# Second mixer: mLSTM output with tokens on partitions, and the large products of a beat in one run

## What is computed

```python
Dm = jnp.where(causal, b[..., :, None] - b[..., None, :] + ig[..., None, :], -jnp.inf)
m = jnp.maximum(bq, jnp.max(Dm, axis=-1))
Wt = jnp.exp(Dm - m[..., None]) * jnp.einsum('bhcld,bhcsd->bhcls', qc, kc)
num = inter[..., None] * jnp.einsum('bhcld,bhcdv->bhclv', qc, Cs) + jnp.einsum('bhcls,bhcsv->bhclv', Wt, vc)
den = inter * jnp.einsum('bhcld,bhcd->bhcl', qc, ns) + jnp.sum(Wt, axis=-1)
h = num / jnp.maximum(jnp.abs(den), jnp.exp(-m))[..., None]
```

## Time and profile before

| | us |
|---|---|
| median of 3 runs | 1571.99 (1571.65 to 1573.32) |
| profiled execution | 1571.24 |
| its span | 1569.5 |
| TensorE busy | 1549.0, 99% |
| VectorE busy | 1001.8, 64% |
| ScalarE busy | 705.1, 45% |
| GpSimd busy | 180.9, 12% |

### The profile page before, as it was taken

One profiled execution on the slowest core, in us unless ns is written; L12 is line 12 of the kernel. 1 busy time (PEld: TensorE's weight loads), 2 busy tenths in 40 slices (PEclk: granted clock), 3 DMA queues, 4 the chain that ended last, 5 costly groups with the idle time before them and its releaser, 6 DMA issues.

```text
span 1569.5 us, 20966 instructions
## 1 busy us (share of the span) xinstructions
PE 1549.0 (99%) x7858; PEld 1266.9 (81%) x7858; DVE 1001.8 (64%) x1861; ACT 705.1 (45%) x1386; POOL 180.9 (12%) x167
## 2 busy tenths in 40 slices
PE   8999999999999999999999999999999999999998
PEld 8888888888876888888888888767667888888887
DVE  7876667544778577767653377676776655554356
ACT  7544444423556555444442343344444443433254
POOL 0221122100004202221120000000011011110000
PEclk9999999999999999999999999999999999999999
DMA  5333333334151313333333424221101333333332
GB/s 212 94 104 93 100 101 95 107 95 141 56 151 25 98 38 108 94 100 90 98 101 94 143 95 137 68 48 48 48 28 61 95 93 100 95 98 98 95 113 68
DMA packets 91973, 146.21 MB, mean 93 GB/s; under 512 B 9056, under 2 KB 30944, under 8 KB 91744
## 3 DMA queue, kind: packets, MB, share of 16 engines
q1 hardware_dynamic: 89392, 139.07, 29.8%
q10 hardware_dynamic: 2480, 5.80, 1.2%
HBM read 140.12 MB, written 2.10 MB: 91 GB/s over the span
## 4 chain that ended last, share of the span: by engine, by line
PE 91%; DVE 5%; issue 1%; ACT 1%; DMA 1%; SPq 0%; POOL 0%; DVEq 0%; POOLq 0%
PE ps L452 24%; PE ps L454 24%; PE ps L453 24%; PE ps L2039 2%; PE ps L2041 1%; PE ps L2040 1%; PE ps L491 1%; PE ps L492 1%; PE ps L493 1%; PE ps L1763 1%; PE ps L1743 1%; PE ps L1722 1%; PE ps L1378 1%; PE ps L1409 1%; PE ps L473 1%
## 5 line engine op out<-in xcount | busy, mean ns | idle before, releaser
L437 DVE TENSOR_TENSOR wl<-raw,wh 128x512 fp32r<-128x512 f32 (+2 forms) x419 | 303.7, 729 | 391.5 <-ACT wh L428 390.7
L428 ACT ACTIVATE wh<-raw 128x512 fp32r<-128x512 f32 (+2 forms) x419 | 260.8, 627 | 539.3 <-PE ps L454 534.5
L452 PE MATMUL ps<-Hh,wh 128*128 128x512 f32 x1088 | 426.1, 392 | 2.2 <-DVE st L1830 1.9
L454 PE MATMUL ps<-Hh,wl 128*128 128x512 f32 x1088 | 423.5, 389 | 0.0
L453 PE MATMUL ps<-Hl,wh 128*128 128x512 f32 x1088 | 423.4, 389 | 0.0
L452 PEld LDWEIGHTS ps<-Hh,wh 128*128 128x128 f32 x1088 | 204.1, 188 | 46.0 <-DVE Hl L2328 2.1
L454 PEld LDWEIGHTS ps<-Hh,wl 128*128 128x128 f32 x1088 | 204.1, 188 | 42.8
L453 PEld LDWEIGHTS ps<-Hl,wh 128*128 128x128 f32 x1088 | 204.2, 188 | 42.0
L452 PE MATMUL ps<-AH,wh 128*128 128x512 f32 x416 | 161.8, 389 | 0.0
L453 PE MATMUL ps<-AL,wh 128*128 128x512 f32 x416 | 161.8, 389 | 0.0
L454 PE MATMUL ps<-AH,wl 128*128 128x512 f32 x416 | 161.8, 389 | 0.0
(11 more groups left out here) (352 smaller groups left out, 2236.3 us busy)
## 6 DMA issues: line engine op xcount, KB each, us to landing
raw<-in_w_in SPq DMA_DIRECT2D x216, 256.0 KB, 2.7
raw<-in_w_out SPq DMA_DIRECT2D x104, 256.0 KB, 2.6
raw<-in_w_up SPq DMA_DIRECT2D x64, 256.0 KB, 2.7
raw<-in_w_down SPq DMA_DIRECT2D x32, 256.0 KB, 2.7
raw<-in_w_q SPq DMA_DIRECT2D x16, 256.0 KB, 2.8
raw<-in_w_o SPq DMA_DIRECT2D x16, 256.0 KB, 3.2
raw<-in_w_pg SPq DMA_DIRECT2D x16, 256.0 KB, 2.6
X<-in_xT SPq DMA_DIRECT2D x8, 256.0 KB, 4.6
```

Of the source, the lines that this page charges most:

```text
L428: e.activation(split_in[n][0][:, 0:width], raws[n % NRAW][:, 0:width], ACT.Copy, scale=1.0 if gain is None else gain).then_inc(s_hi, 1)
L437: e.tensor_tensor(wl[:, 0:width], raw, wh[:, 0:width].bitcast(F32), ALU.subtract).then_inc(s_lo, 1)
L452: e.matmul(b, wh[:, o:o + w], xh, start=k == 0, stop=False, skip_group_check=joined)
L454: m = e.matmul(b, wl[:, o:o + w], xh, start=False, stop=k == (nk - 4 if closing else nk - 1), skip_group_check=joined)
```

## The change

The output of an mLSTM head is now made with tokens on partitions: the decayed scores are the weights and the values are streamed, with a column of ones beside them (`mvt` is 129 of 132 wide), so that the sum of the weights comes out as column 128. Blocks 0 to 2 of tokens go to bank 3, block 3 (step 5) to bank 2. The squares are summed by ScalarE with `accum_out`; the two Abs follow. `dve_lstm_diag` scales the rows on VectorE (384 and 128 columns of PSUM), and step 7 transposes the four blocks back, after which VectorE multiplies with the gate out of PSUM. The additions on GpSimd and VectorE, the products with ones and the copy of the output go away.

TensorE's order in a beat is `unit`, `sums`, both groups of transposes, the `lstm` step, and then all large products of the beat. Thirty beats hold two halves, four hold one, beats 34 and 35 none; the `lstm` steps begin in beat 6. VectorE takes a tile at the start of the next beat. All tiles of the inputs go to bank 0. Bank 1 is for the transposes of group 1; units with one or two blocks put both groups into bank 6, and ScalarE copies both at once. Head 3's output moves ahead of the attention's last two in the order of `w_out`.

```diff
+        mvt = sub("b_mvt", [P, 2, 4, 132], o_)
...
-        W_ORDERS = ((0, 1, 4, 5, 6, 2, 3, 7), (0, 1, 2, 4, 5, 6, 3, 7))
+        W_ORDERS = ((0, 1, 4, 5, 6, 7, 2, 3), (0, 1, 2, 4, 5, 6, 3, 7))
...
-        M_FIRST = {b: ("m", b, 0) for b in range(29)}
-        M_SECOND = {b: ("m", b, 1) for b in range(29)}
-        M_SECOND.update({29 + i: ("m", 29 + i // 2, i % 2) for i in range(6)})
...
-            MIX += second_half + [("turn", b)] + [("mtake", t // 2)] * (t % 2 and half) + step
-            if b >= 8 and (b % 8 < 2 and b < 32 or b in (34, 35)):
-                MIX += [("mo", b // 8 - 1, b % 8 % 2)]
+            at_ = sum(RUN[:b])
+            run = halves[at_:at_ + RUN[b]] if b < NU else [("w0", b - NU)]
+            lane = b - LSTM_AT
+            step = [("lstm", *LSTM[lane])] if 0 <= lane < 32 else []
+
+            MIX += made + [("unit", b)]
+            MIX += [("lstm_diag", lane // 8)] * (0 <= lane < 32 and lane % 8 == 7)
+            MIX += [("lstm_exp", *LSTM[lane - 1])] * (1 <= lane <= 32 and (lane - 1) % 8 < 4)
+            MIX += run + [("turn", b)] + step
+            if lane >= 3 and (lane % 8 in (3, 4) and b < 30 or b in (35, 36)):
+                MIX += [("mo", 3 if b > 30 else lane // 8, (lane + 1) % 2 if b < 30 else b - 35)]
             if b > 32:
                 MIX += [("fill", b - 33)]
-
-            if b < 5:
-                PE_MIX += (first_half if b == 0 else []) + [("unit", b)] + (first_half if b else [])
-                PE_MIX += [("turn0", b)] + second_half + [("turn", b)]
-            elif b < 29:
-                PE_MIX += [("unit", b), ("sums", b), ("turn0", b)] + first_half + den + [("turn", b)] + second_half + step
+            made = [("mtake", t // 2) for what, t, half in run if t % 2 and half] if b < NU else []
+
+            if b == 0:
+                PE_MIX += run[:1] + [("unit", b)] + run[1:]
+            elif b < 5:
+                PE_MIX += [("unit", b)] + run + [("turn", b)]
             elif b < NU:
-                PE_MIX += [("unit", b), ("sums", b), ("turn0", b)] + den + second_half + [("turn", b)] + step
+                PE_MIX += [("unit", b), ("sums", b), ("turn", b)] + step + run
             else:
-                PE_MIX += [("w0", b - 35)] * (b == NU + 2) + [("turn0", b), ("sums", b)] + den
-                PE_MIX += second_half + [("turn", b)] + step
-        MIX += [("lstm_diag", 3), ("fill", 6), ("w0", 4), ("w0", 5), ("lstm", *LSTM[31]), ("w0", 6), ("fill", 7), ("w0", 7)]
-        PE_MIX += [("w0", 4), ("w0", 5), ("lstm", *LSTM[31]), ("w0", 6), ("w0", 7)]
+                PE_MIX += [("sums", b), ("turn", b)] + step + run
+        MIX += [("w0", 3), ("fill", 6), ("w0", 4), ("fill", 7), ("w0", 5), ("w0", 6), ("w0", 7)]
+        PE_MIX += [("w0", c) for c in range(3, 8)]
...
+        def short(u):
+
+            return u >= 4 and UNITS[u][1] < 2
...
+        def turn_bank(u, g):
+
+            return turned[6][:, 256 * g:] if short(u) else turned[(6, 1)[g]]
...
                 tb = UNITS[u][1]
+                bank = turn_bank(u, g)
                 if g == 0:
                     e.wait_ge(s_nm, u + 1)
                     if u > 0:
-                        e.wait_ge(s_cp1, u)
-                else:
-                    e.wait_ge(s_cp0, u + 1)
+                        e.wait_ge(s_cp0, u)
+                elif not short(u) and second_copies(u) > 1:
+                    e.wait_ge(s_cp1, second_copies(u) - 1)
...
-                    e.activation(unit_t(u, 0)[:, 0:L], turned[6][:, 0:L], ACT.Copy).then_inc(s_cp0, 1)
+                    if short(u):
+                        i = (0, 4)[u % 2]
+                        e.activation(tall[:, i:i + 2, 2:2 + L], turned[6].rearrange("p (g c) -> p g c", g=2)[:, :, 0:L],
+                                     ACT.Copy).then_inc(s_cp0, 1)
+                    else:
+                        e.activation(unit_t(u, 0)[:, 0:L], turned[6][:, 0:L], ACT.Copy).then_inc(s_cp0, 1)
...
+            if 0 <= u < NU and not short(u):
                 tb = UNITS[u][1]
...
         LT, LB, LN = [T[2], T[3], T[6], T[7]], turned[2], turned[3]
-        DECAY = (LT[1], LT[2], LT[3], LT[2])
...
                 e.wait_ge(s_mm, 4 * h + i + 1)
                 if i == 0:
                     e.wait_ge(s_mtc, h + 1)
-                e.matmul(LN[:, n0:S], mvt[:, h, i, :], DECAY[i][:, n0:S], start=i == 0, stop=i == 3,
-                         skip_group_check=True).then_inc(s_ma, 1)
-            if s == 6:
-                e.wait_ge(s_msq, h + 1)
+                for tb in range(i, 3):
+                    m = e.matmul(LN[:, LD * tb:LD * tb + LD], DECAY[i][:, (tb - i) * P:(tb - i + 1) * P],
+                                 mvt[:, h % 2, i, 0:LD], start=i == 0 and tb == 0, stop=i == tb, skip_group_check=True)
+                if i == 2:
...
+            if s == 5:
+                e.wait_ge(s_mm, 4 * h + 4)
+                for i in range(4):
+                    m = e.matmul(LB[:, 0:LD], DECAY[i][:, (3 - i) * P:(4 - i) * P], mvt[:, h % 2, i, 0:LD], start=i == 0,
+                                 stop=i == 3)
+                m.then_inc(s_ma, 1)
+            elif s == 7:
+                e.wait_ge(s_mrow, h + 1)
                 for tb in range(4):
-                    m = e.matmul(LB[:, 8 + tb:9 + tb], LT[2][:, tb * P:(tb + 1) * P], ones[:, 0:1], start=False,
-                                 stop=True, skip_group_check=True)
-                m.then_inc(s_mden, 1)
-            elif s == 7:
-                e.wait_ge(s_mdx, h + 1)
-                for tb in range(4):
...
-                e.activation(mvt[:, h, :, :], LN[:, :].rearrange("p (n c) -> p n c", n=4), ACT.Copy).then_inc(s_mtc, 1)
...
-                e.wait_ge(s_mres, h + 1)
-                e.activation(LT[2], big[:, MQ + h, :], ACT.Square).then_inc(s_msq, 1)
-            elif s == 6:
-                e.wait_ge(s_mden, h + 1)
                 if h > 1:
-                    e.wait_ge(s_mdx, h - 1)
-                e.activation(lane_col(h, 0), LB[:, 0:4], ACT.Abs).then_inc(s_mabs, 1)
+                    e.wait_ge(s_mrow, h - 1)
+                for tb in range(4):
+                    if tb % 3 == 0:
+                        e.wait_ge(s_ma, 2 * h + 1 + tb // 3)
+                    e.activation(LT[(3, 1)[tb // 2]][:, tb % 2 * P:(tb % 2 + 1) * P], l_rows(tb), ACT.Square, accum_out=lane_col(h, 2)[:, tb:tb + 1])
+                e.activation(lane_col(h, 0)[:, 0:3], LN[:, 0:3 * LD].rearrange("p (b c) -> p b c", b=3)[:, :, P], ACT.Abs)
+                e.activation(lane_col(h, 0)[:, 3:4], LB[:, P:LD], ACT.Abs).then_inc(s_mabs, 1)
...
-            if s in (3, 4):
-                i = s - 2
-                n0 = i * P
-                e.wait_ge(s_mm, 4 * h + i + 1)
-                e.wait_ge(s_ma, 4 * h + 1)
-                if i == 2:
-                    e.wait_ge(s_mc, 2 * h + 1)
-                e.tensor_tensor(LT[1][:, n0:S], LT[1][:, n0:S], DECAY[i][:, n0:S], ALU.add).then_inc(s_mc, 1)
             if s < 4:
-                n0 = s * P
...
-                e.wait_ge(s_mm, 4 * h + 4)
-                e.tensor_tensor(LT[1][:, 3 * P:S], LT[1][:, 3 * P:S], DECAY[3][:, 3 * P:S], ALU.add).then_inc(s_mc3, 1)
-                e.wait_ge(s_ma, 4 * h + 4)
-                e.tensor_copy(big[:, MQ + h, :], LN[:, :]).then_inc(s_mres, 1)
...
-                e.tensor_tensor(big[:, MQ + h, :], big[:, MQ + h, :], big[:, MO + h, :], ALU.mult).then_inc(s_mt, 1)
             elif s == 7:
                 e.wait_ge(s_mbr, h + 1)
-                e.wait_ge(s_mt, h + 1)
...
-                e.tensor_tensor(big[:, MQ + h, :], big[:, MQ + h, :], LB[:, :], ALU.mult).then_inc(s_mn, 1)
+                e.wait_ge(s_mg, h + 1)
+                e.tensor_tensor(big[:, MQ + h, :], LB[:, :], big[:, MO + h, :], ALU.mult).then_inc(s_mn, 1)
         def dve_lstm_diag(e, h):
...
+            e.wait_ge(s_mdx, h + 1)
+            e.tensor_tensor(LT[1][:, 0:3 * P].rearrange("p (b c) -> p b c", b=3),
+                            LN[:, 0:3 * LD].rearrange("p (b c) -> p b c", b=3)[:, :, 0:P],
+                            c1[:, 0:3].unsqueeze(2).to_broadcast([P, 3, P]), ALU.mult)
+            e.tensor_scalar(LT[1][:, 3 * P:S], l_rows(3), c1[:, 3:4], None, ALU.mult).then_inc(s_mrow, 1)
         s_mdx, s_mg = sem("l_divisor"), sem("l_gate")
...
-            b = turned[t // 2 % 2][:, :]
+            b = turned[0][:, :]
...
+                        e.wait_ge(s_mev, t // 2)
                     multiply_m(e, t, half)
```

More of the change, by code:

```diff
@@ L1625, in build @@
         MIX += [("take", 2)]
-        M_FIRST = {b: ("m", b, 0) for b in range(29)}
-        M_SECOND = {b: ("m", b, 1) for b in range(29)}
-        M_SECOND.update({29 + i: ("m", 29 + i // 2, i % 2) for i in range(6)})
+        RUN = [2] * 30 + [1, 1, 1, 1, 0, 0]
+        LSTM_AT = 6
         PE_MIX = list(MIX)
+        halves = [("m", t, half) for t in range(32) for half in range(2)]
+        made = []
         for b in range(NU + 3):
[L1634 to L1644, removed]
```

(47 more changed lines are left out.)

48 lines of the change are left out of this document (14 added, 34 removed).

## The result

The kernel after the change takes 1577.3 us (median of six runs, 1575.1 to 1580.1); the kernel before took 1572.0 beside it (1571.6 to 1573.3). The ratio is 1.0033 [1.0023, 1.0043]: 5.3 us slower, 0.34%, which is more than a measurement can confuse with no change. The prediction was 1572.6 with a range of 1566 to 1578. The time lies in the range and on the side that was given 0.29; the forecast, no change, did not come. The profiled execution of after is the slowest of its six, 1580.1 us with a span of 1578.4, so its parts add up to more than the median shows (8.9 us between the two spans, 5.3 between the medians).

A forecast was written before the change was run, and what follows sets the result against it. TensorE was taken to bound the kernel (busy 99% of the span, 91% of the chain), its queue packed. Terms: -6.9 - 1.05 + 5.3 + 1.2 + 2.05 = +0.6, so 1572.6 us, range 1566 to 1578.

The forecast's parts named there:

- the side that was given 0.29: Whole kernel: the outcome slower than before by more than 0.2%, chance 0.29.
- (1) to (4): TensorE's queue: one-column products -6.5, turned output product +0.2, divisor transposes nothing, large products together -0.6; sum -6.9 us.
- C: Rival: loads of the new output products aren't hidden, 2.0 us more per head, +8, 1580.6; chance 0.04.
- (4): TensorE's large products together in one run per beat: 0.02 us saved a beat, 0.6 in 30 beats.
- D: Rival: putting the large products together saves nothing for changing over, +0.6, 1573.2; chance 0.06.
- 0.35 stalls: TensorE, beat after each of the first three heads begins: stalls of about 0.35 us go, -1.05 in all.
- (5): TensorE ahead of step 7 in beats 13, 21, 29: new waits for VectorE's row scaling, 1.3, 1.9, 2.1 us; +5.3.
- A: Rival: the waits of (5) and (7) don't come or only in small part; -10, 1562, half 1567; chance 0.20.
- B: Rival: clock falls behind beat 37's wait, threshold between 1.95 and 5.4 us at rest; +2.9, 1574.9; chance 0.20.
- (6): Inputs in one bank: TensorE waits for VectorE's take, 0.95 in beat 2, 1.05 in beat 4; net +1.2 with memset.
- beat 5's 1.17: TensorE's rest of 1.17 us in beat 5 of the kernel before, forecast to go.
- (7): Mixer's end: waits of 1.5 us in beats 34 to 36 and last unit, 3.8 ahead of last step 7; net +2.05.

The follow-up runs named there:

- step 7 behind: Changed kernel with only step 7 of each head (the four transposes back) moved behind the beat's large products: 1564.5 us, ratio 0.9956.
- both moves: Changed kernel with step 7 behind the large products in all four beats and the transposes of beats 2 to 4 ahead of them: 1560.6 us, 0.9922.
- filled waits: Changed kernel with needless 128x128 products on TensorE ahead of its long waits (beats 2, 4 and the four step 7), result wrong: 1573.2 us, 1.0008.
- early transposes: Changed kernel with the transposes of beats 0 to 4 ahead of the large products instead of behind both halves: 1573.0 us, 1.0003.
- the second bank: Changed kernel with the second tile of the mLSTM inputs in bank 7, so a product waits for one take fewer: 1572.7 us, 1.0004.

## Why the prediction was off, by its own steps

**(1) to (4), the work.** Taken at -6.9; the remainder above is -6.35. The same account (length of the mixer less rests, against before) gives -7.1 for the kernel with step 7 behind (213.99 us, of which 5.2 are rests) and -6.7 for the one with both moves (210.54, 1.3), and there is no half clock in the mixer of either. So the term is right within what the account can tell. The products with ones are gone and cost what the earlier trace rows said or a little more (1.68 for 16 passes, against 2 x 0.79). The new output products cost what the nearest row gave, 0.11 a pass, and the four lines below, one for each step and together the 20 passes of a head, make 2.24 against the 2.2 forecast; C, loads that aren't hidden, is excluded:

```profile
1088.55 0.67 PE ps L1934 x6
...
1093.62 0.45 PE ps L1934 x4
...
1099.29 0.23 PE ps L1934 x2
```
```profile
1058.60 0.89 PE ps L1941 x8
```

Whether the 0.6 of (4) is among it, the account is too coarse to say. The better test is the kernel with all steps behind the large products: one more change-over in most beats costs it under 0.1 us in all against step 7 alone, where 0.02 a beat would be some 0.5. That speaks for D, that putting large ones together saves nothing, on this term.

**The 0.35 stalls** are gone, as forecast: in after's chain the twelve large products of the beats that answer to the earlier trace rows's 1084.84 (from 1082.91 and from 1089.22) follow each other at 0.23 from the first to the last.

**(5), step 7 in beats 13, 21 and 29.** Forecast 1.3, 1.9 and 2.1; measured 1.30, 1.92 and 2.10. VectorE's rows in beat 21 are the sum in order: scores, normalising, divisor, 384 columns, 128 columns, and 0.06 later TensorE starts.

```profile
1114.29 0.42 DVE L1844 CUSTOM_DVE_ANT_0 b_Sb<-ps,b_bias 128x256 f32<-128x256 f32 x1 [0.62 <-PE ps L1718]
...
1115.38 0.61 DVE L1876 TENSOR_SCALAR b_Sb<-b_Sb,st 128x256 f32<-128x256 f32 x2
1115.91 0.16 DVE L2018 SCALAR_TENSOR_TENSOR st<-st 128x4 f32<-128x4 f32 x1
1116.10 0.56 DVE L2020 TENSOR_TENSOR t_all<-ps,st 128x384 f32<-128x384 f32 x1
1116.57 0.34 DVE L2023 TENSOR_SCALAR t_all<-ps,st 128x128 f32<-128x128 f32 x1
```

A, that these waits don't come, is excluded for (5). But the step stopped at the wait: it gave no thought to what TensorE's clock does behind it, although its 1.9 and 2.1 lie at and above the one rest that B used as its lower end.

**(6), inputs in one bank.** Beat 2 is right, 0.96 against 0.95. Beat 4 is mis-sized: 2.42 against 1.05. The step allowed 0.3 for the transposes behind both halves, as a delay of the copies alone, and left out what is queued behind a copy on ScalarE: the rounding of the next weights, on which VectorE waits. The lag was 1.5 instead of 0.3. And beat 5's 1.17 did not go, 0.89 of it stayed. Together +3.1 where +1.2 stood.

**(7), the end.** Forecast +2.05 in rests; measured about +0.45 (0.40 + 2.99 against the 0.98 + 1.95 that before's trace shows here; the prediction's 1.15 + 2.1 has small waits with it that aren't counted in after either). Beats 34 to 36 have one wait of 0.40, not four of 1.5 in all. Ahead of step 7 it is 2.99, not 3.8, since the squares of ScalarE start 0.25 apart, not 0.39, and the first ones run before the last output products are done:

```profile
1195.38 0.28 ACT L1962 ACTIVATE t_all<-ps 128x128 f32<-128x128 f32 x1
...
1195.63 0.29 ACT L1962 ACTIVATE t_all<-ps 128x128 f32<-128x128 f32 x1
...
1196.38 0.21 ACT L1963 ACTIVATE st<-ps 128x3 f32<-128x3 f32 x1
```
```profile
1199.88 0.16 DVE L2001 TENSOR_TENSOR st<-st 128x4 f32<-128x4 f32 x1
...
1202.80 0.34 DVE L2023 TENSOR_SCALAR t_all<-ps,st 128x128 f32<-128x128 f32 x1
```

From the last output product to the scaled rows it is 7.4 us, where 8.2 to 8.4 were forecast, and TensorE's own work in it 4.4, as forecast.

**The sum without the clock.** The errors of (6) and (7), +1.9 and -1.6, nearly cancel: rests +7.8 against +7.5 forecast (-1.05 + 5.3 + 1.2 + 2.05). With the work, -6.35 against -6.9, that makes +1.45 against +0.6. At full clock the forecast "no change" would have held, as the kernel with filled waits bears out (1.0008 [0.9998, 1.0018]), and that part of it was luck in two of the sum's five terms.

**B, the step that failed.** The clock was made a rival with one place, beat 37, with a price of 2.3 and a chance of 0.20. It fell behind 2.99 us there, and cost 2.7. But it fell in two more places, behind 2.42 and 1.92 us, for 1.6 and 1.55. The error is in the bound: "between 1.95 and 5.4 us at rest" took one rest that went well for a rest that is safe. In the mixers of these eleven traces, a rest of 1.3 us or less never brought it; 1.92 brought it in after and in the kernel with early transposes, not in that with the second bank; 2.10 brought it in the second bank's and the early transposes' but not in after's; 1.95 didn't in before; 2.42 in two traces of four; 2.99 to 3.00 in all four. The length of one rest isn't the whole of it: near the start of the program the clock fell in five of the eleven, where the longest rest close ahead was 0.84 us. The Trainium skill (TensorE: Matmul & The Clock Gate, Part 1: The HAM clock gate) says that the clock halves after an idle stretch and comes back under sustained work; the trace agrees as to the mixer, with the stretches of 3.4 and 6.9 us at 0.50 behind rests shown above, and 1.00 after them. Priced as it came, with a fall behind the longer half of the waits of (5) and (6) as well, the sum would have been 1572.6 + 5.85, or 1578.5, and the side of the forecast another.

In one sentence: the waits were found and nearly all sized rightly, their sum was right by luck, and what they do to the clock, 4 to 6 us, was counted in one place and at one chance in five.

## What to carry to other kernels

Price a new wait on a packed TensorE twice: its length, and, from about 2 us on, some 1.5 us or more at half clock that can come behind it, in each place where such a wait comes and not only in the longest. Put a product that needs another engine's work of the same beat behind the beat's independent products: here the move of four such items was worth 12.8 us, more than the whole arithmetic saved (some 6.5). And where transposes are held back, follow what is queued behind their copy on the copying engine: the copy was 0.6 us, but the weight split behind it made the wait.

## What the runs showed of the hardware

- The fall of the clock isn't a fixed function of the rest ahead of it. Kernels that differ only elsewhere, with the same rests to 0.01 us, had it behind different ones, and this makes a spread: after's six runs lie 5.1 us apart, the ten of the kernel with filled waits 1.4, the four of the kernel with both moves 0.8 (before's, timed beside, 1.7 to 3.2 apart). And it came in five traces of eleven near the start of the program, where the longest rest close ahead of it was 0.84 us.
- The fall can come late. In the second bank's kernel TensorE works again from 1196.90 and its first products still go at full pace; the clock is 0.50 only from 1198.0, and for 3.4 us. In after it is at 0.50 already when work begins again behind the same rest, and for 6.8 us. So one rest can cost 1.4 to 1.6 us (three traces) or 2.7.
- An fp32 product over one column costs nearly as much as one over 129: 0.105 a pass for 16 passes, against 0.11. Four output blocks of 129 columns, with the sum of the weights as their last column, therefore got that sum for next to nothing: the transposes of 128 columns take the same 0.11 a pass.
